# A layer norm and the first two FFN chunks in two halves of 256 tokens, the first during the output projection

## The reference

```python
x = layer_norm(ALPHA * x + y @ w_out[l], ln_mix_g[l], ln_mix_b[l])
hg, hu = jnp.split(x @ w_ffn_in[l], 2, axis=-1)          # 1024 -> 2 * 2816
x = layer_norm(ALPHA * x + (jax.nn.silu(hg) * hu) @ w_ffn_out[l], ln_ffn_g[l], ln_ffn_b[l])
```

## Time and profile before

| | |
|---|---|
| median of 3 runs | 870.41 us (868.68 to 871.64) |
| the profiled execution, its own time | 870.8 us |
| its span in the trace | 869.0 us |
| mean granted TensorE clock over the span | 0.991 |
| TensorE busy | 840.9 us (97%) |
| VectorE, ScalarE busy | 506.3 us (58%), 347.5 us (40%) |
| GpSimd busy | 29.1 us (3%) |

### The profile page before, as it was taken

One profiled execution on the slowest core, in us unless ns is written; L12 is line 12 of the kernel. 1 busy time (PEld: TensorE's weight loads), 2 busy tenths in 40 slices (PEclk: granted clock), 3 DMA queues, 4 the chain that ended last, 5 costly groups with the idle time before them and its releaser, 6 DMA issues.

```text
span 869.0 us, 10442 instructions
## 1 busy us (share of the span) xinstructions
PE 840.9 (97%) x4039; PEld 702.4 (81%) x4039; DVE 506.3 (58%) x829; ACT 347.5 (40%) x522; POOL 29.1 (3%) x81
## 2 busy tenths in 40 slices
PE   7999899999999999999999899999999999999995
PEld 4989797888887888888888688888888888888884
DVE  4346778798879887867562586433333333322227
ACT  4354565576545634633341542322222222211112
POOL 2500000000000000000000200000000000000001
PEclk9999999999999999999999999999999999999998
DMA  6542212112212122122235122422222222222202
GB/s 242 176 155 85 97 49 97 49 67 80 85 62 97 49 97 97 50 97 97 92 137 208 48 97 97 146 97 97 97 97 97 97 97 97 97 97 97 97 1 97
DMA packets 14152, 85.01 MB, mean 98 GB/s; under 512 B 1680, under 2 KB 1940, under 8 KB 5280
## 3 DMA queue, kind: packets, MB, share of 16 engines
q1 hardware_dynamic: 11952, 77.34, 24.7%
q0 software_dynamic: 2016, 6.86, 2.3%
q10 hardware_dynamic: 144, 0.26, 0.1%
HBM read 82.33 MB, written 2.13 MB: 97 GB/s over the span
## 4 chain that ended last, share of the span: by engine, by line
PE 86%; DVE 10%; ACT 2%; issue 1%; DMA 1%; POOL 0%; SPq 0%; DVEq 0%; POOLq 0%; ACTq 0%
PE bank L1153 60%; PE bank L1296 17%; PE bank L1259 2%; PE bank L1223 1%; DVE w_lo L763 1%; PE bank L1225 1%; PE bank L1177 1%; DVE sel L840 1%; PE bank L1354 1%; PE bank L1246 1%; DVE top L838 1%; DMA xraw<-in_xT 1%; DVE pT_lo_D L868 1%; ACT w_hi L489 1%; DVE resid L1034 1%
## 5 line engine op out<-in xcount | busy, mean ns | idle before, releaser
L763 DVE TENSOR_TENSOR w_lo<-raw,w_hi 128x2048 fp32r<-128x2048 f32 x69 | 158.1, 2291 | 157.0 <-ACT w_hi L489 134.2
L1153 PE MATMUL bank<-x_lo,w_hi 128*128 128x512 f32 x720 | 184.0, 393 | 0.0
L1153 PE MATMUL bank<-x_hi,w_hi 128*128 128x512 f32 x720 | 179.3, 391 | 0.0
L1153 PE MATMUL bank<-x_hi,w_lo 128*128 128x512 f32 x720 | 178.0, 389 | 0.0
L1153 PEld LDWEIGHTS bank<-x_hi,w_lo 128*128 128x128 f32 x720 | 135.1, 188 | 28.3
L1153 PEld LDWEIGHTS bank<-x_lo,w_hi 128*128 128x128 f32 x720 | 134.5, 189 | 27.1
L1153 PEld LDWEIGHTS bank<-x_hi,w_hi 128*128 128x128 f32 x720 | 134.0, 188 | 27.2
L489 ACT ACTIVATE w_hi<-raw 128x2048 fp32r<-128x2048 f32 x48 | 92.1, 1919 | 105.4 <-PE bank L1296 94.9
L1296 PE MATMUL bank<-w_hi,h_hi 128*128 128x512 f32 x176 | 56.8, 389 | 0.0
L1296 PE MATMUL bank<-w_hi,h_lo 128*128 128x512 f32 x176 | 56.8, 389 | 0.0
L1296 PE MATMUL bank<-w_lo,h_hi 128*128 128x512 f32 x176 | 56.7, 389 | 0.0
(11 more groups left out here) (264 smaller groups left out, 1056.8 us busy)
## 6 DMA issues: line engine op xcount, KB each, us to landing
raw<-in_stream SPq DMA_DIRECT2D x69, 1024.0 KB, 4.8
resid<-in_x POOLq DMA_DIRECT2D x1, 2048.0 KB, 8.2
xraw<-in_xT SPq DMA_DIRECT2D x3, 512.0 KB, 7.8
out<-result SPq DMA_DIRECT2D x3, 512.0 KB, 2.6
bias_b<-bias_vectors POOLq DMA_DIRECT2D x1, 1024.0 KB, 6.9
bias_a<-bias_vectors POOLq DMA_DIRECT2D x1, 1024.0 KB, 12.8
ln_g<-in_g POOLq DMA_DIRECT2D x2, 512.0 KB, 7.4
ln_b<-in_b POOLq DMA_DIRECT2D x2, 512.0 KB, 8.3
```

Source lines behind the costliest of these rows:

```text
L763: dve.tensor_tensor(w_lo[:, s, :], raw[:, s, :], w_hi[:, s, :].bitcast(f32), ALU.subtract).then_inc(lo_ready, 1)
L1153: ins = pe.matmul(dst, lhs[a](k), rhs[b](k), start=n == 0, stop=n == n_all - 1)
```

## The change

The tokens are taken in two halves, tiles 0 and 1, and tiles 2 and 3 (`HALF`). The transposes of a half use four banks instead of eight, two k side by side in each. `turn(0)` stands before (2,3), ahead of the last 24 products of the output projection. The first gate and up chunk are done as four sets of products 256 columns wide: gate half 0, then `turn(1)`, up half 0, gate half 1, up half 1. VectorE's and ScalarE's lists are put in the order that goes with it; on both, the scaling, rounding and subtracting of a half go over 256 columns at a time, 16 instructions instead of 8 for each of the three.

```diff
@@ -74,6 +74,7 @@
           22: 1}
 assert sum(ROUNDS.values()) == 3 * (TOPK // 8)
 MASK_SLOT = 22
+HALF = [slice(0, SEQ // 2), slice(SEQ // 2, SEQ)]
 O_BUF = {"D": 0, "B": 1, "C": 0, "A": 1}
 
 
@@ -701,18 +702,23 @@
                 act.activation(deviation[:, tok % 2, :], resid[:, tok, :], ACT.Square, bias=neg_mean[:, tok:tok + 1],
                                accum_out=squares[:, tok:tok + 1]).then_inc(squares_ready, 1)
 
+            def x1_high(half, first, end):
+
+                for k in range(first, end):
+                    act.wait_ge(x1t_ready, KT * half + k + 1)
+                    act.activation(x_hi[:, k, HALF[half]], x1t[:, k, HALF[half]], ACT.Copy).then_inc(x1_hi_ready, 1)
+
             square(0, 0)
             square(0, 1)
             norm(0)
+            norm(1)
             square(0, 2)
-            norm(1)
+            x1_high(0, 0, KT // 2)
             high(FIN0)
+            norm(2)
+            x1_high(0, KT // 2, KT)
             square(0, 3)
-            norm(2)
             norm(3, D_MODEL // 2)
-            for k in range(KT):
-                act.wait_ge(x1t_ready, k + 1)
-                act.activation(x_hi[:, k, :], x1t[:, k, :], ACT.Copy).then_inc(x1_hi_ready, 1)
 
             def high_of(c, s, loads, used, count):
 
@@ -723,6 +729,7 @@
             def ffn_pair(p, parity, first=False, early=False):
                 if first:
                     high(FIN0 + 1)
+                    x1_high(1, 0, KT)
                 else:
                     high_of(FIN0 + 1 + 2 * p, (FIN0 + 1) % 2, p + (FIN0 + 2) // 2, up_done, 2 * p)
                 for j in range(2):
@@ -1054,26 +1061,43 @@
                 dve.tensor_tensor(shift[:, one], neg_mean[:, one], rstd[:, one], ALU.mult).then_inc(rstd_ready, 1)
 
             dve.wait_ge(resid_loaded, 16)
-            for tok in range(TOK):
-                row_means(mix_done, tok)
-                if tok:
-                    refine(0, tok - 1)
+            def x1_turned(half):
+
+                for k in range(KT):
+                    dve.wait_ge(turned, 4 * half + k // 2 + 1)
+                    first = SEQ // 2 * (k % 2)
+                    dve.tensor_scalar(x1t[:, k, HALF[half]], banks[4 * half + k // 2][:, first:first + SEQ // 2], g1_col[:, k:k + 1],
+                                      b1_col[:, k:k + 1], ALU.mult, ALU.add).then_inc(x1t_ready, 1)
+
+            def x1_low(half, first, end):
+
+                for k in range(first, end):
+                    dve.wait_ge(x1_hi_ready, KT * half + k + 1)
+                    dve.tensor_tensor(x_lo[:, k, HALF[half]], x1t[:, k, HALF[half]], x_hi[:, k, HALF[half]].bitcast(f32),
+                                      ALU.subtract).then_inc(x1_lo_ready, 1)
+
+            row_means(mix_done, 0)
+            row_means(mix_done, 1)
+            refine(0, 0)
+            refine(0, 1)
+            row_means(mix_done, 2)
+            dve.wait_ge(cols_loaded, 32)
+            x1_turned(0)
+            refine(0, 2)
+            x1_low(0, 0, KT // 2)
+            row_means(mix_done, 3)
             low(FIN0)
+            x1_low(0, KT // 2, KT)
             refine(0, TOK - 1)
             dve.wait_ge(rstd_ready, TOK)
             v = resid[:, TOK - 1, D_MODEL // 2:]
             dve.tensor_scalar(v, v, rstd[:, TOK - 1:TOK], shift[:, TOK - 1:TOK], ALU.mult, ALU.add).then_inc(norm_half_ready, 1)
-            dve.wait_ge(cols_loaded, 32)
-            for k in range(KT):
-                dve.wait_ge(turned, k + 1)
-                dve.tensor_scalar(x1t[:, k, :], banks[k][:], g1_col[:, k:k + 1], b1_col[:, k:k + 1],
-                                  ALU.mult, ALU.add).then_inc(x1t_ready, 1)
-            for k in range(KT):
-                dve.wait_ge(x1_hi_ready, k + 1)
-                dve.tensor_tensor(x_lo[:, k, :], x1t[:, k, :], x_hi[:, k, :].bitcast(f32), ALU.subtract).then_inc(x1_lo_ready, 1)
 
             def ffn_pair(p, parity, first=False, early=False):
                 low(2 * p + (FIN0 + 1), (FIN0 + 1) % 2)
+                if first:
+                    x1_turned(1)
+                    x1_low(1, 0, KT)
                 for j in range(2):
                     dve.wait_ge(tanh_ready, 2 * p + (j + 1))
                     dve.scalar_tensor_tensor(swi[:, j, :], swi[:, j, :], 1.0, banks[4 * parity + j][:], ALU.add,
@@ -1288,7 +1312,21 @@
                     slot_half(t, 0, units)
                     slot_half(t, 1)
 
-            def rows_product(c0, n_chunks, left, chunk_signal, done, left_ready, first_banks_free):
+            def turn(half):
+
+                for tok in (2 * half, 2 * half + 1):
+                    pe.wait_ge(norm_ready, tok + 1)
+                    if half:
+                        pe.wait_ge(mean_ready, TOK)
+                    for k in range(KT):
+                        if tok == TOK - 1 and k == KT // 2:
+                            pe.wait_ge(norm_half_ready, 1)
+                        first = SEQ // 2 * (k % 2) + P * (tok % 2)
+                        ins = pe.transpose(banks[4 * half + k // 2][:, first:first + P], resid[:, tok, P * k:P * (k + 1)], ident[:])
+                        if tok % 2 and k % 2:
+                            ins.then_inc(turned, 1)
+
+            def rows_product(c0, n_chunks, left, chunk_signal, done, left_ready, first_banks_free, before_last=None):
 
                 def tile(j, tok, kk, n, half):
 
@@ -1315,6 +1353,8 @@
                     if tok == 0:
                         pe.wait_ge(lo_ready, c0 + j)
                         pe.wait_ge(left_ready, 2 * j + 2)
+                    if before_last is not None and j == n_chunks - 2 and tok == TOK - 1:
+                        before_last()
                     for half in range(2):
                         for kk in range(2):
                             for n in range(len(PARTS)):
@@ -1329,35 +1369,38 @@
             pe.wait_ge(probsT_ready, stage2_banks_before(len(UNITS)))
             pe.wait_ge(o_lo_ready, HEADS * len(BRANCH_ORDER))
             rows_product(OUT0, KT // 2, (y_hi, y_lo), out_chunk_done, mix_done, y_lo_ready,
-                         lambda: pe.wait_ge(act_emptied, EMPTIED_BY.count("act")))
-
-            pe.wait_ge(mean_ready, TOK)
-            for tok in range(TOK):
-                pe.wait_ge(norm_ready, tok + 1)
-                for k in range(KT):
-                    if tok == TOK - 1 and k == KT // 2:
-                        pe.wait_ge(norm_half_ready, 1)
-                    ins = pe.transpose(banks[k][:, P * tok:P * (tok + 1)], resid[:, tok, P * k:P * (k + 1)], ident[:])
-                    if tok == TOK - 1:
-                        ins.then_inc(turned, 1)
+                         lambda: pe.wait_ge(act_emptied, EMPTIED_BY.count("act")), lambda: turn(0))
+
+            def x1_tiles(which, half):
+
+                w = [columns((FIN0 + which) % 2, P * j, P, CW) for j in range(2)]
+                early, late = range(KT // 2), range(KT // 2, KT)
+                steps = ([(0, 0, k) for k in range(KT)] + [(0, 1, k) for k in early] + [(1, 0, k) for k in range(KT)]
+                         + [(0, 1, k) for k in late])
+                for n, (a, b, k) in enumerate(steps):
+                    pe.wait_ge(x1_lo_ready if b else x1_hi_ready, KT * half + k + 1)
+                    if n == 0:
+                        pe.wait_ge(hi_ready, FIN0 + which)
+                    if n == KT + KT // 2:
+                        pe.wait_ge(lo_ready, FIN0 + which)
+                    for j in range(2):
+                        if n == 0 and half == 0:
+                            pe.wait_ge(x1t_ready, 2 * (2 * which + j + 1))
+                        ins = pe.matmul(banks[2 * which + j][:, HALF[half]], w[j][a](k), (x_hi, x_lo)[b][:, k, HALF[half]],
+                                        start=n == 0, stop=n == len(steps) - 1)
+                        if half and n == len(steps) - 1:
+                            ins.then_inc((gate_done, up_done)[which], 1)
 
             def ffn_pair(p, parity, first=False, early=False):
+                if first:
+                    x1_tiles(0, 0)
+                    turn(1)
+                    x1_tiles(1, 0)
+                    x1_tiles(0, 1)
+                    x1_tiles(1, 1)
+                    return
                 for which, signal, freed in ((0, gate_done, gated), (1, up_done, hidden_ready)):
                     pe.wait_ge(lo_ready, 2 * p + (FIN0 + which))
-                    if first and which == 0:
-                        w = [columns(FIN0 % 2, P * j, P, CW) for j in range(2)]
-                        for k in range(KT):
-                            pe.wait_ge(x1_hi_ready, k + 1)
-                            for a, j in ((0, 0), (1, 0), (0, 1), (1, 1)):
-                                if k == 0 and a == 0:
-                                    pe.wait_ge(x1t_ready, j + 1)
-                                pe.matmul(banks[j][:], w[j][a](k), x_hi[:, k, :], start=k == 0 and a == 0, stop=False)
```

(6 more changed lines are left out.)

## The result

The changed kernel took 864.61 us (median of 8 runs, 862.44 to 866.99), the kernel before 870.65 (8 runs, 868.68 to 872.0): a ratio of 0.9935, 95% interval 0.9918 to 0.9951, that is 4.3 to 7.1 us less. The forecast was 866.2 (864.4 to 869.1) against 870.4. The profiled execution took 866.78 with a span of 865.0, against 870.8 and 869.0 before: there the difference is 4.0.

What follows compares the result with a forecast made beforehand. TensorE, busy 97% of the span, was taken as the bound. Of 6.5 us to win, width took 1.3 and waits 0.2 + 0.6 + 0.1: 4.3, by clock times 4.1, taken as 4.2; forecast 866.2 us, range 864.4 to 869.1.

Steps and rivals of the forecast that it cites:

- loss on k 4 to 7 of `x_hi`: Gate half 0: TensorE loses 0.2 us on ScalarE's roundings of k 4 to 7, ready at 494.5.
- wait for the gate split: Gate half 0: TensorE, after 24 products, waits 0.6 us for VectorE's `low(FIN0)`, queued behind tile 3's means.
- wait ahead of the up chunk: Before up half 0: TensorE waits 0.1 us for ScalarE's `high(FIN0 + 1)`, queued behind tile 3's normalization.
- next pair: The gate and up chunks after the first pair: TensorE starts them at 518.4 on the old time axis, 522.54 before.
- gain at the place: Up to the end of the first up chunk: 4.3 us by terms, 4.1 by clock times, taken as 4.2.
- The ceiling of 6.5: Between output projection and first gate and up chunks: at most 4.9 us idle plus 1.6 us half clock can be won.
- The width: First gate and up chunks: 192 products of 256 columns at 0.120 replace 96 of 512, a loss of 1.3 us.
- GpSimd locked out for longer: Rival, 0.18: tile 3's variance gets no turn between VectorE's subtractions, all behind moves 0.85 us; gain 3.3, 867.1.
- The clock falls all the same: Rival, 0.12: transposes between 495 and 501.1 are no clock activity, half clock costs 1.6 us; gain 2.6, 867.8.
- Waits between narrow products: Rival, 0.07: a wait at each of 96 narrow steps costs time; at 0.08 us each 7.7 in all, 873.9.
- Given back later: Rival, 0.05: behind 518, `low` of one of the next two chunks is 1 to 2 us late; gain 2.7, 867.7.
- the cover left: Next gate chunk: its tanhs, `high` and `low` take 5.3 us under a last set of 5.76, 0.4 to spare.

Runs made afterwards that it cites:

- late transposes in the same lists: Changed kernel with the transposes of tiles 0 and 1 behind the output projection's last product: 872.08 against 869.73 before, ratio 1.0019.
- four profiles with fillings: Kernel before, with overwritten products or transposes in TensorE's idle time between real transposes, each profiled twice: 869.03 and 869.78 us against 869.73.
- the run with narrow products everywhere: Kernel before, with every FFN input product except the first gate chunk's done as two of 256 columns: 883.31 us, ratio 1.0155.

## Why the prediction was right

Step by step, the predicted starts moved by the 0.35 us of the square:

| step | predicted | measured |
|---|---|---|
| `turn(0)` without a wait | 485.6 | 485.60 |
| first gate product | 492.85 | 492.80 |
| loss on k 4 to 7 of `x_hi` | 0.2 | 0.3 (16 products in 2.21, 1.92 without) |
| wait for the gate split | 0.6 | 0.41 idle, 0.55 by starts |
| `turn(1)` | 499.5 | 499.47 |
| wait ahead of the up chunk | 0.1 | none shown |
| gate, half 1 | 507.25 | 507.00 |
| next pair | 518.75 | 518.52 |
| gain at the place | 4.2 | 4.4 |

- **The mechanism was the forecast's**: late transposes in the same lists lose the whole gain, with waits of 3.7 and 0.4. The two tenths by which the place won more than forecast are mostly TensorE's transposes: 16 took 1.66 and 1.70 by starts, where the sum had 1.8 each time.
- **The ceiling of 6.5** was read rightly as what TensorE loses in all, but its two terms do not stand alone: 4.9 idle and 1.6 clock. Alone the clock is worth 1.0, because VectorE's subtractions and the next split were just hidden by the slower products. The prediction did not see this. The sum came out all the same, since the change moves those too.
- **The width** cost what the row of the same form said, 0.120 a product; measured a second time over 21 chunks, 13.4 us.
- **GpSimd locked out for longer** (0.18) did not happen: the variance took 0.59 and ended within 0.05 us of the split, although VectorE went on with two-input subtractions. Of the two readings the one in the forecast was right.
- **The clock falls all the same** (0.12) did not happen, and four profiles with fillings show that transposes held the clock in this gap as products did. The rule of the Trainium skill (TensorE: Matmul & The Clock Gate, Part 4: PE-mode transpose), that a transpose does not count as busy in the way a product does, finds no support here: two of the four fillings were transposes only, with 1.00 from 488 to 508 in the one and from 488 to 506 in the other. The page's times there are for bf16, the transposes here are f32. How they would do in a long run of nothing else was not tried.
- **Waits between narrow products** (0.07) cost nothing: the sets with a wait at each of 24 steps take 5.76, the narrow groups without such waits 0.96 for eight, the same 0.120.
- **Given back later** (0.05) did not happen either; the cover left, put at 0.4, was 0.47.
- The median, 864.6, lay 1.6 under the forecast. That is not a term of the sum: repeated, it was 866.1. In the profiles the clock fell, apart from the place of the change and the end, only near 12, 107 and 274 us, and not in all of them; for runs without a trace only the mean is known. The prediction's 0.5 for this spread was small, and it was luck that the first median still lay in the range, by 0.2.

## What to carry to other kernels

Where a dependent chain on the vector engines stands bare between two blocks of products, splitting the tokens and starting the chain under the last products of the first block can close most of the gap: here 4.4 of 6.5 us, 1.3 of the rest being paid for the narrower products, which are counted by a row of their own width. Once the gap was closed here, the next wait was within half a microsecond, and reordering moved it from place to place. Compare traces from an event ahead of the change to the end: here this gave 386.4 in both profiles, where single runs spread over 4.5 us and more.

## What the runs showed of the hardware

- Products of 256 columns follow each other at 0.120 us, of 512 at 0.2267: half the columns cost 53% of the time, measured over 2016 products of the run with narrow products everywhere (13.4 us more).
- A fall of the clock need not cost what the slower products take longer: 1.5 us longer products (7.36 at full clock, 8.87 at half for part of them), 1.0 us at the end.
- Ahead of the change the clock differs from run to run of the same kernel: the one with products as filling ran at half clock from 12.2 to 15.6 us in its first profile, from 12.1 to 18.9 and from 107.7 to 111.1 in its second.
- A one-column GpSimd instruction that met VectorE's split of 2048 columns, an instruction with two SBUF inputs, took 1.60 (before), 0.59 (changed) and 0.88 us (transposes late) instead of 0.19, and ended each time 0.05 to 0.06 after the split. In the last two, further instructions with two SBUF inputs followed directly and did not hold it longer.
